# Two residual blocks on one Trainium2 core: the normalised activations' two halves are kept in two regions instead of side by side

## What is computed

```python
def rmsnorm_2(x, g):
    x32 = x.astype(jnp.float32)
    y = x32 * lax.rsqrt(jnp.mean(x32 * x32, axis=-1, keepdims=True) + EPS)
    return (y * g.astype(jnp.float32)).astype(x.dtype)

def swiglu(x, w_in, w_out):                      # three of these, d_ff 2816
    gate, up = jnp.split(x @ w_in, 2, axis=-1)
    return (jax.nn.silu(gate) * up) @ w_out
...
h = swiglu(rmsnorm_2(x, norm_ffn1_pre[l]), w_ffn1_in[l], w_ffn1_out[l])
x = x + FFN_RESIDUAL_SCALE * rmsnorm_2(h, norm_ffn1_post[l])
h = mixer(rmsnorm_2(x, norm_mix_pre[l]), w_mix_in[l], ...)
```

## Time and profile before

| | us |
|---|---|
| median of three runs | 797.41 |
| the profiled execution | 797.35 |
| its span, first to last instruction | 795.6 |
| what lies around the span | 1.75 |

### The profile page before, as it was taken

How to read it: one execution, slowest core, us unless ns; L and a number is a source line. 1 busy time by engine, 2 the same in 40 slices (tenths; PEclk the granted TensorE clock), 3 DMA queues, 4 the chain that set the end, 5 groups by cost and what they waited for, 6 DMA issues and landing times.

```text
span 795.6 us, 12209 instructions
## 1 busy us (share of the span) xinstructions
PE 785.1 (99%) x4710; PEld 693.8 (87%) x4710; DVE 533.2 (67%) x628; ACT 429.5 (54%) x565; POOL 28.3 (4%) x35
## 2 busy tenths in 40 slices
PE   9999999999999999999999999999999999999997
PEld 8989979888888888888888887999988888888885
DVE  7865567766666667866666566766977766666665
ACT  6556658444544548744544446565557644454444
POOL 0000000000000000000000000002420000000000
PEclk9999999999999999999999999999999999999999
DMA  9633333655555543665555554452444655555521
GB/s 335 232 115 117 140 110 139 229 182 187 205 172 203 184 185 110 238 227 192 202 171 208 180 189 158 140 204 108 160 167 165 218 217 175 194 198 175 208 105 54
DMA packets 20797, 141.16 MB, mean 177 GB/s; under 512 B 2448, under 2 KB 2704, under 8 KB 4384
## 3 DMA queue, kind: packets, MB, share of 16 engines
q1 hardware_dynamic: 20192, 138.65, 49.0%
q0 software_dynamic: 576, 2.10, 0.8%
HBM read 139.69 MB, written 1.05 MB: 177 GB/s over the span
## 4 chain that ended last, share of the span: by engine, by line
PE 94%; DVE 2%; ACT 2%; issue 1%; DMA 1%; SPq 0%; DVEq 0%; ACTq 0%
PE ps L1466 93%; ACT whi L683 1%; PE ps L1472 1%; DMA raw<-wstream 1%; DVE x L1215 0%; ACT squared L698 0%; DVE xa L1022 0%; PE ps L1695 0%; DVE wlo L1011 0%; PE ps L1665 0%; PE ps L1915 0%; DVE xg L1210 0%; DVEq L271 0%; ACT L916 0%; PE ps L1697 0%
## 5 line engine op out<-in xcount | busy, mean ns | idle before, releaser
L1466 PE MATMUL ps<-xa,whi 128*128 128x512 f32 (+2 forms) x1744 | 376.1, 346 | 0.0
L1011 DVE TENSOR_TENSOR wlo<-raw,whi 128x2048 fp32r<-128x2048 f32 x128 | 293.7, 2295 | 82.2 <-ACT whi L683 82.1
L1466 PEld LDWEIGHTS ps<-xa,whi 128*128 128x128 f32 x1744 | 300.2, 188 | 40.0 <-issue 2.1
L683 ACT ACTIVATE whi<-raw 128x2048 fp32r<-128x2048 f32 x128 | 244.1, 1908 | 6.9 <-PE ps L1466 6.8
L1466 PE MATMUL ps<-xa,wlo 128*128 128x256 f32 (+1 forms) x1376 | 225.7, 283 | 0.0
L1466 PEld LDWEIGHTS ps<-xa,wlo 128*128 128x128 f32 x1376 | 193.6, 191 | 2.4
L1466 PE MATMUL ps<-whi,hhi 128*128 128x512 f32 x240 | 93.4, 389 | 0.0
L1466 PE MATMUL ps<-wlo,hhi 128*128 128x512 f32 x240 | 93.4, 389 | 0.0
L1466 PE MATMUL ps<-whi,hlo 128*128 128x512 f32 x240 | 93.4, 389 | 0.0
L863 ACT ACTIVATE arena<-ps 128x512 f32<-128x512 f32 x33 | 19.7, 596 | 87.1 <-PE ps L1466 87.1
L877 ACT ACTIVATE hhi<-arena 128x512 fp32r<-128x512 f32 x30 | 19.0, 632 | 88.1 <-PE ps L1466 81.6
(11 more groups left out here) (221 smaller groups left out, 531.5 us busy)
## 6 DMA issues: line engine op xcount, KB each, us to landing
raw<-wstream SPq DMA_DIRECT2D x128, 1024.0 KB, 4.8
gain_row<-rows_in POOLq DMA_DIRECT2D x4, 512.0 KB, 3.9
x<-x_in SPq DMA_DIRECT2D x2, 512.0 KB, 4.0
raw<-wstream SPq DMA_DIRECT2D x2, 512.0 KB, 5.6
out<-x SPq DMA_DIRECT2D x4, 256.0 KB, 2.1
xg<-const_in SPq DMA_DIRECT2D x1, 912.0 KB, 13.0
small<-small_in SPq DMA_DIRECT2D x1, 152.0 KB, 6.0
arena<-meta_in SPq DMA_DIRECT2D x1, 64.0 KB, 4.6
```

The source lines that it names most:

```text
L683: nc.scalar.activation(whi[slot][:], raw[slot][:], ACT.Copy).then_inc(hi_ready, 1)
L1011: nc.vector.tensor_tensor(wlo[slot][:], raw[slot][:], whi[slot][:].bitcast(F32), ALU.subtract).then_inc(lo_ready, 1)
L1466: return nc.tensor.matmul(o, lhsT, rhs, start=start, stop=stop, skip_group_check=True)
```

## The change

It gives each of the four views two regions, one for all lo blocks and one for all hi blocks. In a region the eight blocks follow each other at 1024 bytes. The two numbers of `XN_AT` are the start of the view and the distance of the second region, in values of 4 bytes. With `XN_HI = (1, 1, 1, 1)` the second region is hi's in all four. So for k = 0, 1 and 3 lo starts at 0 and hi at 2128 values, that is 8512 bytes = 8192 + 320. For k = 2 lo starts at 32 values, which is 128 bytes, and hi at 2128 values again. The 512-column products move the two regions' blocks as one access of two pieces of 256 values, lo first; their result has whi·lo in the first half of the bank and whi·hi in the second. The other products read the same blocks as before at their new places. The `xa` of the first block stays as it was.

```diff
-XN_AT = (0, 0, 80, 0)
+XN_AT = ((0, 2128), (0, 2128), (32, 2096), (0, 2128))
+XN_HI = (1, 1, 1, 1)
...
-        xn = [xa_line[:, c:c + KT * 2 * SEQ].rearrange("p (k c) -> p k c", k=KT) for c in XN_AT]
+        for at, far in XN_AT:
+            line = xa_line[:, at:at + KT * 2 * SEQ if far == SEQ else at + 2 * far]
...
+                xn.append(line.rearrange("p (h r) -> p h r", h=2)[:, :, 0:KT * SEQ].rearrange("p h (k c) -> p k h c", k=KT))
+        xn_hi = [xn[k][:, :, n, :] for k, n in enumerate(XN_HI)]
+        xn_lo = [xn[k][:, :, 1 - n, :] for k, n in enumerate(XN_HI)]
...
-                    nc.scalar.activation(xn[k][:, kt, 0:SEQ], turn_place(k, kt), ACT.Copy, scale=vec(gain, kt)).then_inc(xa_hi_ready, 1)
+                    nc.scalar.activation(xn_hi[k][:, kt, :], turn_place(k, kt), ACT.Copy, scale=vec(gain, kt)).then_inc(xa_hi_ready, 1)
...
-                        xn[k][:, kt, SEQ:2 * SEQ], turn_place(k, kt), vec(gain, kt),
-                        xn[k][:, kt, 0:SEQ].bitcast(F32), ALU.mult, ALU.subtract).then_inc(xa_ready, 1)
+                        xn_lo[k][:, kt, :], turn_place(k, kt), vec(gain, kt),
+                        xn_hi[k][:, kt, :].bitcast(F32), ALU.mult, ALU.subtract).then_inc(xa_ready, 1)
...
-                            ins = mm(ps[:, bank + a, :], whi[slot][:, w], xn[norm][:, kt, 0:2 * SEQ], start and kt == 0, not start and kt == KT - 1)
+                            ins = mm(two(bank + a), whi[slot][:, w], xn[norm][:, kt, :, :], start and kt == 0, not start and kt == KT - 1)
...
-                            ins = mm(ps[:, bank + a, 0:SEQ], wlo[slot][:, w], xn[norm][:, kt, 0:SEQ], start and kt == 0, not start and kt == KT - 1)
+                            ins = mm(ps[:, bank + a, 0:SEQ], wlo[slot][:, w], xn_hi[norm][:, kt, :], start and kt == 0, not start and kt == KT - 1)
```

More of the change, by code:

```diff
@@ L420, in build_blocks @@
         xa_line = xa[:].rearrange("p k c -> p (k c)")
-        xn = [xa_line[:, c:c + KT * 2 * SEQ].rearrange("p (k c) -> p k c", k=KT) for c in XN_AT]
+        xn = []
+        for at, far in XN_AT:
+            line = xa_line[:, at:at + KT * 2 * SEQ if far == SEQ else at + 2 * far]
+            if far == SEQ:
+                xn.append(line.rearrange("p (k h c) -> p k h c", k=KT, h=2))
+            else:
+                xn.append(line.rearrange("p (h r) -> p h r", h=2)[:, :, 0:KT * SEQ].rearrange("p h (k c) -> p k h c", k=KT))
+        xn_hi = [xn[k][:, :, n, :] for k, n in enumerate(XN_HI)]
+        xn_lo = [xn[k][:, :, 1 - n, :] for k, n in enumerate(XN_HI)]
+        xa_hi, xa_lo = xa[:, :, 0:TOK], xa[:, :, TOK:2 * TOK]
         ps_line = ps[:].rearrange("p b c -> p (b c)")
@@ L1489, in spread_rstd, with columns_tile @@
                 ins.then_inc(rstd_spread, 1)
-            def columns_tile(o, slot, a, of, n, skip=0):
+            def columns_tile(o, slot, a, of_hi, of_lo, skip=0):
                 for kt in range(KT):
                     w = slice(kt * 256 + a * P, kt * 256 + (a + 1) * P)
-                    mm(o, whi[slot][:, w], of[:, kt, skip:n], kt == 0, False)
-                    mm(o, whi[slot][:, w], of[:, kt, n + skip:2 * n], False, False)
-                    ins = mm(o, wlo[slot][:, w], of[:, kt, skip:n], False, kt == KT - 1)
+                    mm(o, whi[slot][:, w], of_hi[:, kt, skip:], kt == 0, False)
+                    mm(o, whi[slot][:, w], of_lo[:, kt, skip:], False, False)
+                    ins = mm(o, wlo[slot][:, w], of_hi[:, kt, skip:], False, kt == KT - 1)
                 return ins
@@ L1508, in first_paired_unit @@
                         w = slice(kt * 256 + a * P, kt * 256 + (a + 1) * P)
-                        mm(ps[:, bank + a, 0:SEQ], whi[slot][:, w], xn[k][:, kt, 0:SEQ], kt == 0, False)
-                        mm(ps[:, bank + a, 0:SEQ], wlo[slot][:, w], xn[k][:, kt, 0:SEQ], False, False)
+                        mm(ps[:, bank + a, 0:SEQ], whi[slot][:, w], xn_hi[k][:, kt, :], kt == 0, False)
+                        mm(ps[:, bank + a, 0:SEQ], wlo[slot][:, w], xn_hi[k][:, kt, :], False, False)
                 for kt in range(KT):
@@ L1514, in first_paired_unit @@
                         w = slice(kt * 256 + a * P, kt * 256 + (a + 1) * P)
-                        ins = mm(ps[:, bank + a, SEQ:2 * SEQ], whi[slot][:, w], xn[k][:, kt, SEQ:2 * SEQ], False, kt == KT - 1)
+                        ins = mm(ps[:, bank + a, SEQ:2 * SEQ], whi[slot][:, w], xn_lo[k][:, kt, :], False, kt == KT - 1)
                 return ins
@@ L1529, in first_columns_unit @@
                         w = slice(kt * 256 + c, kt * 256 + c + P)
-                        mm(o, whi[slot][:, w], xn[k][:, kt, 0:SEQ], kt == 0 and c == 0, False)
-                        mm(o, wlo[slot][:, w], xn[k][:, kt, 0:SEQ], False, False)
+                        mm(o, whi[slot][:, w], xn_hi[k][:, kt, :], kt == 0 and c == 0, False)
+                        mm(o, wlo[slot][:, w], xn_hi[k][:, kt, :], False, False)
                 for kt in range(KT):
@@ L1535, in first_columns_unit @@
                         w = slice(kt * 256 + c, kt * 256 + c + P)
-                        ins = mm(o, whi[slot][:, w], xn[k][:, kt, SEQ:2 * SEQ], False, kt == KT - 1)
+                        ins = mm(o, whi[slot][:, w], xn_lo[k][:, kt, :], False, kt == KT - 1)
                 return ins
             def tokens_tile(o, slot, tt):
-                hi, lo = slice(tt * P, (tt + 1) * P), slice(SEQ + tt * P, SEQ + (tt + 1) * P)
+                t = slice(tt * P, (tt + 1) * P)
                 for kt in range(KT):
                     w = slice(kt * 256, (kt + 1) * 256)
-                    mm(o, xn[2][:, kt, hi], whi[slot][:, w], kt == 0, False)
-                    mm(o, xn[2][:, kt, hi], wlo[slot][:, w], False, False)
-                    ins = mm(o, xn[2][:, kt, lo], whi[slot][:, w], False, kt == KT - 1)
+                    mm(o, xn_hi[2][:, kt, t], whi[slot][:, w], kt == 0, False)
+                    mm(o, xn_hi[2][:, kt, t], wlo[slot][:, w], False, False)
+                    ins = mm(o, xn_lo[2][:, kt, t], whi[slot][:, w], False, kt == KT - 1)
                 return ins
@@ L1643, in _ @@
                         skip = META if query else 0
-                        columns_tile(ps[:, i % 2, skip:TOK], n % SLOTS, i % 2, xa, TOK,
+                        columns_tile(ps[:, i % 2, skip:TOK], n % SLOTS, i % 2, xa_hi, xa_lo,
                                      skip).then_inc(unit_used if i % 2 else even_full, 1)
@@ L1865, in _ @@
                                 ins.then_inc(mgate_done, 1)
-                            ins = columns_tile(ps[:, bank, a * SEQ:(a + 1) * SEQ], n % SLOTS, a, xn[2], SEQ)
+                            ins = columns_tile(ps[:, bank, a * SEQ:(a + 1) * SEQ], n % SLOTS, a, xn_hi[2], xn_lo[2])
                     ins.then_inc(unit_used, 1)
@@ L1871, in _ @@
                     for kt in range(KT):
-                        for part in range(2):
-                            ins = mm(ps[0:BACK + 16, 2, 0:SEQ], gate_w[:, kt, :], xn[2][:, kt, part * SEQ:(part + 1) * SEQ],
-                                     kt == 0 and part == 0, kt == KT - 1 and part == 1)
+                        mm(ps[0:BACK + 16, 2, 0:SEQ], gate_w[:, kt, :], xn_hi[2][:, kt, :], kt == 0, False)
+                        ins = mm(ps[0:BACK + 16, 2, 0:SEQ], gate_w[:, kt, :], xn_lo[2][:, kt, :], False, kt == KT - 1)
                     ins.then_inc(mgate_halves, 1)
```

## The result

The changed kernel takes 801.65 us (median of five runs, 801.35 to 802.11) against 797.64 us for the kernel before beside it; the ratio is 1.0049, 95% interval 1.0036 to 1.0062. The forecast was 789.0 us, with a range up to 795.6. The profiled execution took 802.02 us with a span of 800.1, which is 4.5 us more than before.

A forecast was written before the change was run, and what follows sets the result against it. TensorE's matmul pace was taken to bound the kernel. From 797.35 us, 7.4 less for short products and 1.0 less for long ones gave 788.95, predicted as 789.0 us, range 786.8 to 795.6.

The forecast's parts named there:

- What bounds the kernel: TensorE, busy for 99% of the span: the pace of its matmuls sets the time, and faster matmuls show in full.
- Short products: 1152 256-column products of the feed-forward networks, hi now at 320 bytes: from 119.7 to 113.3 ns, 7.4 us less.
- the nearest row: Trace row chosen to forecast the short products' pace: the second mixer's first unit, alternating two weight tiles, at 113.3 ns.
- Long products: 1008 512-column products: steady pace stays at 226.7 ns; 33 runs after short ones gain 0.03 us each, 1.0 us less.
- the jump: Between the two pieces of each of 1008 long products: taken as nothing, bounds 0 to 7 ns each, 0 to 7 us.
- My theory: Moving and stationary operands at equal residues modulo 512 bytes collide, so moving hi to 320 bytes quickens short products.
- rows 11: Trace row of a product moving two pieces of 128 columns, 0.12 us; read as showing no cost of a jump.
- The mixer and the writes: Second mixer's products and the writes of hi and lo at new places: nothing; writes within 0.6 us each way.
- The slow pace at 320: Rival: short runs take 117.8 ns, as `columns_tile` does; 795.2 us, perhaps 794.2; chance 0.13.
- the jump costs: Rival: two-piece long products lose 3 to 7 ns each, the rest as forecast; 792 to 796 us; chance 0.07.
- My rival for slower: Restart of the moving read at column 257 costs 13 ns in each of 1008 long products; 802.1 us; chance 0.08.
- Nothing moves: Rival: the short products' 119.7 ns comes from something else the two stages don't share; time stays 797.4 us; chance 0.12.

## Why the prediction was wrong

- **What bounds the kernel** was right. The change showed as pace and nothing else, and no wait took its place.
- **Short products: 7.4 us less, at 113.3 ns.** They went to the other pace that I had read from the earlier trace rows, 117.8 ns, which I had priced at 2.2 us less; 5.3 us of the forecast were not there. The step that failed is the choice of the nearest row: I took the mixer's first unit, because it alternates its tiles as these runs do, and I trusted that they begin out of steady long products. That unit is entered from small products of 128 columns and a pause. In the change the long ones themselves stepped between 0 and 320 bytes, and with that step taken out (two regions, both at 320) the short runs took 113.4. With all views at 320 the pace of 113.4 came, with the same alternation of tiles, so the alternation was not what decided. Nor was the load's duration a sign: it is 188 ns at 117.8 too, in the short run of the changed kernel from 209.1 to 212.3 us. Which run falls into which pace stays open; that the way in has a part in it is shown, by this pair and by the first groups, whose runs took the other pace in two of three networks in the changed kernel and in all three with all views at 320.
- **Long products: "226.7 stays", the jump 0 to 7 us.** They went to 232.5 and 233.1 ns: 16 of them 0.09 and 0.07 us longer, 30 x 0.16 + 3 x 0.07 = 5.0 us, where I had counted 1.0 us less. This is the largest miss. The step that failed is the argument that the second half moves when the load is through and so costs nothing wherever it lies: with the first half at 0, a second half at 448 bytes, which is 192 modulo 256, makes 16 of them 3.68 us instead of 3.63, and one at 320 3.72. My theory also had the sign of the place wrong for them. It held equal residues to be the bad case, and long products are at their 226.7 ns just there, and 3 ns slower each at 320, where the short ones gain. The size lay within the bounds that I had given "the jump", and yet it is not the jump: two pieces 8192 bytes apart at one residue cost nothing. It is the step of residue. The row I took for nothing, rows 11, could not show it: both its pieces are the same 128 columns, so its residue does not step.
- **`down`** I had held to be untouched. It took 0.05 us more per group, 30 x 0.05 = 1.5 us, all of it in its first 12 products. Its own places are unchanged, so this is again the way in; how the products ahead of it reach into it is not shown.
- **The mixer and the writes: nothing.** Nearly right. The mixer's new places alone gave 797.84 against 797.45, and the writes took 483 and 477 ns. But the quick unit of `tokens_tile` went from 113.3 to 118.3 ns in the changed kernel, 0.2 us, within the bounds. Its place is not what decides there: with all views side by side at 320, where the mixer's own addresses are those of before, it took 117.8, and with two regions at 320 113.3 again.
- **The rivals** each held one part of what happened. "The slow pace at 320" and "the jump costs" came true together, the second for another reason than the jump. My rival for slower wanted 13 ns per long product because it let the short ones gain in full; that its 802.1 lies so near to 801.65 is luck, since the restart over a distance, its mechanism, cost nothing. From 797.4, 30 x 0.06 = 1.8 us less for the short runs, 5.0, 1.5 and 0.2 more, and 0.3 less for the 144 short products outside the runs of 32 that read hi (2 ns each, an estimate), give 802.0. The two short runs at 113.4 take 0.3 off, 801.7 against 801.65 measured, though the rounding of the rows alone allows 0.3 either way. I had treated the unknown costs as exclusive cases, though the step in the long products brought both, so that the two together deserved a chance of their own.
- **"Nothing moves"** was the forecast of the Trainium skill's sentence on two independent read ports (TensorE: Matmul & The Clock Gate, Part 2). The runs decide against "nothing moves": with form, order and load the same, moving from 0 to 192 bytes took a short product from 119.8 to 113.5 ns, and the load from 192 to 188. They don't show whether it is the ports that the two reads share.

## What to carry to other kernels

For products like these (float32r, a load for each product of 256 or 512 columns), the distance of the moving block from the weight tile, modulo 256 bytes, was worth up to 5% of their pace, and it is free to choose. It has opposite signs for the two lengths, so both have to be counted: all at 320 won 3.6 us here, all at 192 nothing. A sweep of residues appended to the kernel gives a table in one run, but the pace of a run also depends on what ran ahead of it, so the choice has to be measured in the whole kernel. Keep one residue through all the products that follow each other, inside an access of several pieces as well. And price a change of place for every product that reads the block or comes after it, not only for those that it is meant for.

## What the runs showed of the hardware that was not expected

- The pace depends on move less load modulo 256 bytes: blocks of 60 products took 10.45 or 10.46 us at all four equal residues, and 10.26 to 10.58 us elsewhere. The distance does not fix the pace by itself: at distances of 64 and 192 the blocks fell into two groups, 0.13 to 0.16 us apart.
- In steps of 64 bytes, long products of 512 columns are at 3.63 us for 16 only with distance 0; at 64 bytes they take 3.68, at 128 and 192 3.72 and 3.73. Short ones of 256 columns take 119.8 ns at 0, 118.5 to 120 at 128, and 113.3 or 117.8 at 64 and 192. No distance in these steps is best for both. At 240 bytes one long run of 16 was at 226.7 ns as well, entered from short products, and the one ahead of them at 233; what a whole kernel would do there was not tried.
- One and the same run of short products has two paces, 113.3 and 117.8 ns. Within one kernel some runs were at the one and some at the other: 28 and 2 of 30 in the changed kernel. In the sweep, at 112 bytes, one changed from the slow to the quick after 11. What happens inside the chip, a bank or a buffer, no run here shows.
